# The scan stage of a hybrid diffusion step on one Trainium2 core: decay sums spread over the partitions by TensorE, exponentials with a bias on ScalarE, one 1024-column product on VectorE

## The chip, the cores and the metric

The kernel runs on one core of a Trainium2 chip. The core has five engines that run side by side, each with its own instruction stream in order: TensorE (PE: matmuls; its weight loads, PEld, are a row of their own in the profile), VectorE (DVE), ScalarE (ACT), GpSimd (POOL) and SyncE (SP, which issues most DMAs). They meet only in semaphores. The metric is the device time of one execution in microseconds, lower is better; the median of three runs before is 1650.7 us (1649.86 to 1651.47).

## The reference, cut to what matters

One layer works on 640 tokens (128 context, 512 latent), 5 chunks of 128. The stage that is changed is the two-way Mamba-2 scan: 32 heads of 64 columns in 4 groups of 8, state size 128. Per chunk, head and direction it computes

```
a_cs = cumsum(a)                                   # a = dt * a_neg, over the 128 tokens of a chunk
decay[t, s] = exp(a_cs[t] - a_cs[s])  for s <= t, else 0
y_diag = ((C B^T)[t, s] * decay[t, s]) @ (x * dt)  # 128x128 matrix per head and direction
y_off  = (C @ h_in) * exp(a_cs)                    # state that came into the chunk
state  = B^T @ (x * dt * exp(a_end - a_cs));  h = h * exp(a_end) + state
y = y_forward + y_backward + x * d_skip
```

The backward direction is the same with the tokens reversed, so its matrix is non-zero for s >= t. The rest of the layer (gMLP, convolution, projections, the mixture of experts) is not touched.

## The kernel before

The kernel is a chain of stages, each a block that begins and ends with a barrier of all engines: gMLP, branch A, convolution, gates, the scan (`stage_ssd`, L865), the norm behind it, branch B, the output projection, routing, the experts, and the combination. Order inside a stage is written out by hand, engine by engine, with semaphore counts.

The scan stage has a first part of 20 state products (L1029 and L1026, with POOL and DVE weighting rows of X, L936, and DVE carrying states, L1163 and L1166), and then a loop over 40 steps ("subs"): chunks 4, 3, 2, 1, 0, four groups each, and two halves `q` of 4 heads. What one step j does:

- POOL, `decays` (L983): two products 128x512, the low parts of a times a triangular mask, forward and backward. ACT, `decays` (L1121): eight copies 128x128 of the mask scaled with a rounded a, the high parts.
- PE, `prepare(j)` (L1040): four matmuls with 512 columns in one bank; they give a_cs[t] - a_cs[s] for 4 heads, both triangles in one 128x512 tile. Every second step it also makes C B^T of the group (L1048). PE does `prepare(j+1)` before it finishes step j.
- DVE, `masks` (L1197, L1198): C B^T times the lower and the upper mask, every second step. ACT exponentiates the bank (L1133) and scales the one mask product by dt of the forward direction (L1137, four times); DVE adds the other times dt of the backward direction (L1233, four times) and multiplies with the exponentials (L1239): the combined matrix M of 4 heads for both directions.
- PE: the state part C @ h of both directions (L1090, L1091), not in the last 8 steps (chunk 0), then waits for `matrix_ready` and makes y with M as the stationary operand (L1095, four matmuls of 128 columns, each on the X of two heads, of which one half is used). An f32 matmul shows as two records in the profile.
- DVE, `take_y`: scales the state part (L1212), adds (L1217, L1222); POOL makes x * d_skip (L1006) and the last sum into X (L989).

Two more jobs are threaded into the loop: 12 state products of the backward direction (L1029, with L936, L1163, L1166) and 19 of the 24 pieces of the modulation vector (`modulate`, L1059 with 8 f32 matmuls of a 2-column stationary operand, L1061, and the copy L1172 on DVE), which depend on nothing else in the loop but share PSUM bank 4 with C B^T: `modulate` waits for `cb_masked`.

## Time and profile before

| what | before |
|---|---|
| median of 3 runs | 1650.7 us |
| profiled execution, its own time | 1647.13 us |
| its span | 1645.4 us |
| mean granted TensorE clock | 0.913 of full |
| PE / PEld / DVE / ACT / POOL busy in the span | 1369.0 / 1188.6 / 920.8 / 693.6 / 279.6 us |
| the scan's loop: start of its first L1040, start of its last L1095 | 717.79 us, 960.47 us |

The span is from the first to the last instruction; the profiled execution's own time is 1.7 us longer. The granted clock is the share of full speed at which TensorE ran: it has two levels, full (2.4 GHz) and half (1.2 GHz), and a mean between them says how much of a stretch was at either. Matmuls are pipelined, so the distance between the starts of two blocks tells what one of them takes from PE, rather than the duration printed with it. A row of the timeline that has xN joins N records of one line. In the waits, the engine and line on the left sat idle until the engine and line on the right released it.

### The profile page before, as it was taken

The numbers are of one execution on the slowest core, as the hardware profiler recorded it, in microseconds if no ns is written. First come the engines' busy times: TensorE is split into PE (matmuls) and PEld (weight loads), VectorE is DVE, ScalarE is ACT, GpSimd is POOL, SyncE is SP. The second block draws the span as 40 slices with busy tenths as digits, with TensorE's granted clock in tenths as the row PEclk, the third lists the DMA queues.
The fourth block names the chain that finished last, engine by engine and source line by source line (L and its number), as shares of the span: only waits on it lengthen the run. The fifth ranks groups of instructions, "written<-read, shape, count | busy, mean of one in ns | idle before, by whom it ended". The sixth has DMA issues, their size and how long they took to land. (4 is left out here: it accounts for less than half of the span.)

```text
span 1645.4 us, 20520 instructions
## 1 busy us (share of the span) xinstructions
PE 1369.0 (83%) x7697; PEld 1188.6 (72%) x7697; DVE 920.8 (56%) x1201; ACT 693.6 (42%) x1186; POOL 279.6 (17%) x286
## 2 busy tenths in 40 slices
PE   3999989799998999787778734999974489999980
PEld 1799989799997889645555523998873378888860
DVE  2411532476762111288889868233346189999966
ACT  2423311244342221335557747111121177777753
POOL 0600000000000010256667741000004000000002
PEclk9999999899999999898889966999966799999995
DMA  9972211121213331511111131332435589999945
GB/s 385 406 305 77 76 53 52 59 74 57 78 52 109 118 134 72 170 52 39 39 40 40 51 140 60 115 101 92 162 153 195 201 314 408 406 412 413 413 186 204
DMA packets 55498, 267.96 MB, mean 163 GB/s; under 512 B 7467, under 2 KB 11763, under 8 KB 35062
## 3 DMA queue, kind: packets, MB, share of 16 engines
q1 hardware_dynamic: 42806, 221.21, 35.8%
q0 software_dynamic: 12608, 45.62, 7.1%
q8 instruction: 55, 0.90, 0.2%
q14 instruction: 29, 0.24, 0.0%
HBM read 218.54 MB, written 48.27 MB: 162 GB/s over the span
## 5 line engine op out<-in xcount | busy, mean ns | idle before, releaser
L212 PE MATMUL banks<-rounded,rounded 128*128 128x320 f32 (+1 forms) x1168 | 366.5, 314 | 20.2 <-PEq L1266 6.8
L213 PE MATMUL banks<-rounded,rounded 128*128 128x320 f32 (+1 forms) x1168 | 364.5, 312 | 0.0
L214 PE MATMUL banks<-rounded,rounded 128*128 128x320 f32 (+1 forms) x1168 | 364.4, 312 | 0.0
L191 DVE TENSOR_TENSOR rounded<-words,rounded 128x2048 fp32r<-128x2048 f32 x52 | 119.2, 2292 | 226.5 <-ACT rounded L183 224.3
L212 PEld LDWEIGHTS banks<-rounded,rounded 128*128 128x128 f32 (+1 forms) x1168 | 221.5, 190 | 21.8 <-issue 14.4
L1849 DVE TENSOR_TENSOR rounded<-words,rounded 128x2048 fp32r<-128x2048 f32 x93 | 212.9, 2290 | 34.3 <-ACT rounded L1840 33.4
L213 PEld LDWEIGHTS banks<-rounded,rounded 128*128 128x128 f32 (+1 forms) x1168 | 221.5, 190 | 0.4
L214 PEld LDWEIGHTS banks<-rounded,rounded 128*128 128x128 f32 (+1 forms) x1168 | 221.3, 189 | 0.4
L1840 ACT ACTIVATE rounded<-words 128x2048 fp32r<-128x2048 f32 x96 | 183.7, 1917 | 48.0 <-PE banks L1967 40.7
L183 ACT ACTIVATE rounded<-words 128x2048 fp32r<-128x2048 f32 x52 | 99.2, 1909 | 141.0 <-PE banks L233 62.6
L231 PE MATMUL banks<-rounded,rounded 128*128 128x512 f32 x280 | 112.1, 400 | 10.7 <-PEq L632 6.6
L232 PE MATMUL banks<-rounded,rounded 128*128 128x512 f32 x280 | 111.3, 398 | 0.0
L233 PE MATMUL banks<-rounded,rounded 128*128 128x512 f32 x280 | 111.1, 397 | 0.0
L1965 PE MATMUL banks<-rounded,rounded 128*128 128x512 f32 x256 | 103.1, 403 | 2.8 <-issue 2.4
L1966 PE MATMUL banks<-rounded,rounded 128*128 128x512 f32 x256 | 101.5, 397 | 0.0
L1967 PE MATMUL banks<-rounded,rounded 128*128 128x512 f32 x256 | 101.4, 396 | 0.0
L854 POOL DMA_DIRECT2D silu_z<-words x20 | 10.9, 543 | 531.4 <-ACT words L834 531.4
L1121 ACT ACTIVATE rounded<-words,rounded 128x128 fp32r<-128x128 f32 x320 | 97.2, 388 | 0.0
L1233 DVE SCALAR_TENSOR_TENSOR words<-words,words 128x128 f32<-128x128 f32 x160 | 92.6, 636 | 2.6 <-ACT words L1137 2.6
L983 POOL TENSOR_TENSOR rounded<-words,words 128x512 fp32r<-128x512 f32 x80 | 89.1, 1134 | 22.3 <-PE banks L1040 22.3
L1095 PE MATMUL banks<-words,words 128*128 128x128 f32 x320 | 51.2, 310 | 48.2 <-DVE words L1239 48.2
L1095 PEld LDWEIGHTS banks<-words,words 128*128 128x128 f32 x320 | 45.0, 213 | 59.6 <-DVE words L1239 48.2
(269 smaller groups left out, 2227.7 us busy)
## 6 DMA issues: line engine op xcount, KB each, us to landing
words<-in_units SPq DMA_DIRECT2D x52, 1024.0 KB, 5.0
words<-in_wg SPq DMA_DIRECT2D x32, 1024.0 KB, 7.4
words<-in_wu SPq DMA_DIRECT2D x32, 1024.0 KB, 7.5
words<-in_wd SPq DMA_DIRECT2D x32, 1024.0 KB, 8.3
words<-in_w_mod_rest SPq DMA_DIRECT2D x32, 512.0 KB, 4.9
slot_rows<-words POOLq DMA_DIRECT2D x27, 512.0 KB, 22.9
expert_rows<-words POOLq DMA_DIRECT2D x25, 512.0 KB, 9.0
words<-in_w_mod SPq DMA_DIRECT2D x4, 2048.0 KB, 22.5
```

What stands on the lines that cost most here:

```text
L191: self.nc.vector.tensor_tensor(self.lo[:, i % 2, :], self.raw[:, i % 2, :], self.hi[:, i % 2, :].bitcast(F32), ALU.subtract).then_inc(self ...
L212: nc.tensor.matmul(out, lhs[0](k), rhs[0](k), start=(k == 0), stop=False)
L213: nc.tensor.matmul(out, lhs[0](k), rhs[1](k), start=False, stop=False)
L214: last = nc.tensor.matmul(out, lhs[1](k), rhs[0](k), start=False, stop=(k == nk - 1))
L231: nc.tensor.matmul(out, rows[0], w[0][:, k, :], start=(kk == 0), stop=False)
L232: nc.tensor.matmul(out, rows[0], w[1][:, k, :], start=False, stop=False)
L233: last = nc.tensor.matmul(out, rows[1], w[0][:, k, :], start=False, stop=(kk == KD - 1))
L1840: self.nc.scalar.activation(self.hi[:, q % 3, :], self.raw[q], ACT.Copy).then_inc(self.hi_ready, 1)
L1849: (ops or self.nc.vector).tensor_tensor(self.lo[:, q % 3, :], self.raw[q], self.hi[:, q % 3, :].bitcast(F32), ALU.subtract).then_inc(self. ...
L1965: nc.tensor.matmul(o, HB[0][:, kk, :], hi[:, cols], start=(kk == 0), stop=False)
L1966: nc.tensor.matmul(o, HB[0][:, kk, :], lo[:, cols], start=False, stop=False)
L1967: last = nc.tensor.matmul(o, HB[1][:, kk, :], hi[:, cols], start=False, stop=(kk == KD - 1))
```

## The change

The two triangles are no longer put in one tile. For each direction a bank of PSUM first gets a constant from a bf16 matmul of the identity with a tile `shut` (0 where the mask lets through, -BIG elsewhere, 512 columns), and then, per head, an f32 matmul whose stationary operand is one column of a repeated 128 times and whose moving operand is the mask (128 columns): this puts a_cs[t] on all partitions. ACT's exponential then takes the bank with a bias per partition, the negated sum -a_cs[s] (`NCS`, two new copies at the start of the stage), so that exp(a_cs[t] - a_cs[s]) comes out, and 0 outside of the triangle: eight ACT instructions 128x128 per step, into `E`, three steps deep. DVE multiplies all 1024 columns of E with C B^T (`CB`, now a plain copy by ACT out of PSUM) in one instruction. dt goes to the rows of X (`XT`, POOL, `time_rows`, 512 columns per step), and since the two directions have their own matrices and rows, y takes eight f32 matmuls of 64 columns that accumulate in pairs. The high and low parts of a, the masks product, the dt scalings on ACT and DVE and the rounding at the start of the stage are gone. The state part is scaled in one DVE instruction (`scale_off`), taken as soon as PE has made it; POOL adds x * d_skip and the backward state part, and makes the last sum.

```diff
-    RH, RL = kit.rnd(O_HL + 2048, 4, 512), kit.rnd(O_HL + 4096, 4, 512)
-    GX, TT = (kit.at(O_HL + 6144 + 1024 * j, 2, 512) for j in range(2))
+    E = kit.at(O_HL + 2048, 6, 512)
+    XT = kit.at(O_HL + 5120, 6, 256)
...
 PE
             def prepare(j):
                 c, g, q = subs[j]
-                pe.wait_ge(low_decays, 2 * j + 2)
-                if j >= 2:
-                    pe.wait_ge(seg_exp, j - 1)
-                pe.wait_ge(high_decays, 8 * (j + 1))
-                for n, (mask, R) in enumerate(((gtr, RH[:, j % 2, :]), (gtr, RL[:, j % 2, :]),
-                                               (ltr, RH[:, 2 + j % 2, :]), (ltr, RL[:, 2 + j % 2, :]))):
-                    last = nc.tensor.matmul(ps[:, j % 2, :], mask, R, start=(n == 0), stop=(n == 3))
-                last.then_inc(seg_done, 1)
+                for d, mask in ((0, le), (1, ge)):
+                    if j:
+                        pe.wait_ge(decays_done, 8 * j - 4 + 4 * d)
+                    nc.tensor.matmul(ps[:, d, :].rearrange("p (h n) -> p h n", h=4), identb,
+                                     shut[:, d, :].unsqueeze(1).broadcast_to([P, 4, P]), start=True, stop=False)
+                    for h in range(4):
+                        n = 32 * d + heads4(g, q).start + h
+                        last = nc.tensor.matmul(ps[:, d, h * P:(h + 1) * P], A[:, c, n:n + 1].broadcast_to([P, P]), mask,
+                                                start=False, stop=(h == 3))
+                    last.then_inc(sums_spread, 1)
...
+                pe.wait_ge(rows_timed, j + 1)
                 pe.wait_ge(matrix_ready, j + 1)
                 for h in range(4):
-                    x0 = g * GW + q * 256 + (h // 2) * P
-                    last = nc.tensor.matmul(ps[:, 2 + j % 2, h * P:(h + 1) * P], M[:, j % 2, h * P:(h + 1) * P],
-                                            X[:, c, x0:x0 + P], start=True, stop=True)
+                    o = ps[:, 2 + j % 2, h * HD:(h + 1) * HD]
+                    for d in range(2):
+                        b = 2 * (j % 3) + d
+                        last = nc.tensor.matmul(o, E[:, b, h * P:(h + 1) * P], XT[:, b, h * HD:(h + 1) * HD],
+                                                start=(d == 0), stop=(d == 1))
                 last.then_inc(y_done, 1)
...
 ACT
-            nc.scalar.activation(AH, A, ACT.Copy).then_inc(a_split, 1)
             act.wait_ge(sums_done, 1)
+            for n in range(2):
+                nc.scalar.activation(NCS[:, n, :, :].rearrange("p c h -> p (c h)"), ps[:, n, 0:160],
+                                     ACT.Copy, scale=-1.0).then_inc(exps_done, 1)
...
+            for j, (c, g, q) in enumerate(subs):
+                if j >= 3:
+                    act.wait_ge(y_done, j - 2)
+                for d in range(2):
+                    if d and q == 0:
+                        gi = j // 2
+                        act.wait_ge(cb_done, gi + 1)
+                        if gi >= 2:
+                            act.wait_ge(matrix_ready, 2 * (gi - 1))
+                        nc.scalar.activation(CB[:, gi % 2, :], ps[:, 4, (gi % 2) * P:(gi % 2 + 1) * P], ACT.Copy).then_inc(cb_taken, 1)
+                    act.wait_ge(sums_spread, 2 * j + d + 1)
                     for h in range(4):
-                        hs = 32 * d + heads4(g, q).start + h
-                        nc.scalar.activation(RH[:, 2 * d + j % 2, h * P:(h + 1) * P], mask, ACT.Copy,
-                                             scale=AH[:, c, hs:hs + 1].bitcast(F32)).then_inc(high_decays, 1)
+                        n = heads4(g, q).start + h
+                        nc.scalar.activation(E[:, 2 * (j % 3) + d, h * P:(h + 1) * P], ps[:, d, h * P:(h + 1) * P], ACT.Exp,
+                                             bias=NCS[:, d, c, n:n + 1]).then_inc(decays_done, 1)
...
 DVE
-                for h in range(4):
-                    dt = DT[:, c, 32 + g * HPG + 4 * q + h:32 + g * HPG + 4 * q + h + 1]
-                    tt = TT[:, j % 2, h * P:(h + 1) * P]
-                    nc.vector.scalar_tensor_tensor(out=tt, in0=CB[:, (j // 2) % 2, 1, :], scalar=dt, in1=tt,
-                                                   op0=ALU.mult, op1=ALU.add).then_inc(both_scaled, 1)
...
-                nc.vector.tensor_tensor(M[:, j % 2, :], TT[:, j % 2, :], GX[:, j % 2, :], ALU.mult).then_inc(matrix_ready, 1)
+                dve.wait_ge(cb_taken, j // 2 + 1)
+                dve.wait_ge(decays_done, 8 * j + 8)
+                e = E[:, 2 * (j % 3):2 * (j % 3) + 2, :].rearrange("p d (h t) -> p (d h) t", h=4)
+                nc.vector.tensor_tensor(e, e, CB[:, (j // 2) % 2, :].unsqueeze(1).broadcast_to([P, 8, P]),
+                                        ALU.mult).then_inc(matrix_ready, 1)
...
 POOL
+                nc.gpsimd.tensor_tensor(XT[:, 2 * (j % 3):2 * (j % 3) + 2, :].rearrange("p d (h n) -> p d h n", h=4),
+                                        rows.unsqueeze(1).broadcast_to([P, 2, 4, HD]),
+                                        dt.unsqueeze(3).broadcast_to([P, 2, 4, HD]), ALU.mult).then_inc(rows_timed, 1)
```

What this makes of TensorE's instructions in one step of the loop. Before, one step on TensorE, from its `prepare` (L1040) through a state product (L1029), a modulation piece (L1059, L1061), the state part (L1090, L1091) to y (L1095):

```order
L1040 MATMUL banks<-rounded_2048_5415,rounded_128_5417 128x512
L1040 MATMUL banks<-rounded_2048_5416,rounded_128_5417 128x512
L1040 MATMUL banks<-rounded_2048_5415,rounded_128_5418 128x512
L1040 MATMUL banks<-rounded_2048_5416,rounded_128_5418 128x512
L1029 MATMUL banks<-words_52992_59,words_28160_54 128x512
L1059 MATMUL banks<-words_42496_49,words_33280_56 2x128 x8
L1061 MATMUL banks<-words_42496_49,words_52992_59 2x128
L1090 MATMUL banks<-words_10240_52,words_28160_54 128x256
L1091 MATMUL banks<-words_10240_52,words_28160_54 128x256
L1095 MATMUL banks<-words_20480_55,words_50688_5414 128x128 x4
```
After, the same step; L1038 is the bf16 matmul of the constant, L1042 the spread sums, L1030, L1062, L1064, L1094 and L1095 are the old L1029, L1059, L1061, L1090 and L1091, and L1102 is y:

```order
L1038 MATMUL banks<-words_33280_56 128x512
L1042 MATMUL banks<-words_52992_59,words_33280_56 128x128 x4
L1038 MATMUL banks<-words_33280_56 128x512
L1042 MATMUL banks<-words_52992_59,words_33280_56 128x128 x4
L1030 MATMUL banks<-words_52992_59,words_28160_54 128x512
L1062 MATMUL banks<-words_42496_49,words_33280_56 2x128 x8
L1064 MATMUL banks<-words_42496_49,words_52992_59 2x128
L1094 MATMUL banks<-words_10240_52,words_28160_54 128x256
L1095 MATMUL banks<-words_10240_52,words_28160_54 128x256
L1102 MATMUL banks<-words_50688_5414 128x64 x8
```
Nothing has changed its place. Four matmuls of 512 columns have become two of 512 and eight of 128, and four of 128 columns have become eight of 64.

On VectorE, one step and its surroundings before (words_33280_56 holds C B^T, the scales and the state part, words_50688_5414 the exponentials and the matrices):

```order
L1233 SCALAR_TENSOR_TENSOR words_50688_5414<-words_33280_56,words_50688_5414 128x128 x4
L1239 TENSOR_TENSOR words_50688_5414<-words_50688_5414 128x512
L1212 TENSOR_TENSOR words_33280_56<-banks,words_33280_56 128x256 x2
L1217 TENSOR_TENSOR words_42496_49<-banks,words_33280_56 128x2x64 x2
L1222 TENSOR_TENSOR words_42496_49<-words_42496_49,words_33280_56 128x256
L1172 COPY words_42496_49<-banks 2x128
L1163 TENSOR_TENSOR words_42496_49<-words_10240_52,words_33280_56 128x512
L1166 TENSOR_TENSOR words_50688_5414<-words_42496_49,banks 128x512
```
and after, where L1214 is the product, L1194 the scaling of the state part, L1204 the sum that takes y, and L1169, L1160 and L1163 the modulation's copy and the carrying of a state:

```order
L1214 TENSOR_TENSOR words_50688_5414<-words_50688_5414,words_33280_56 128x1024
L1194 TENSOR_TENSOR words_33280_56<-banks,words_33280_56 128x512
L1204 TENSOR_TENSOR words_42496_49<-banks,words_33280_56 128x256
L1169 COPY words_42496_49<-banks 2x128
L1160 TENSOR_TENSOR words_42496_49<-words_10240_52,words_33280_56 128x512
L1163 TENSOR_TENSOR words_50688_5414<-words_42496_49,banks 128x512
```
Ten instructions of a step are three, and the scaling of a step's state part stands ahead of the sum that takes the y of the step before.

On ScalarE at the start of the stage, before:

```order
L1102 ACTIVATE words_33280_56<-words_33280_56 128x16
L1103 ACTIVATE rounded_320_5419<-words_33280_56 128x320
L1106 ACT_TABLE_LOAD
L1106 ACTIVATE words_33280_56<-banks 128x480 x2
L1112 ACTIVATE words_50688_5414<-banks 128x512 x8
```
and after (L1112 are the negated sums, L1115 the exponentials of the sums, L1121 the context states, L1136 the exponentials with a bias):

```order
L1109 ACTIVATE words_33280_56<-words_33280_56 128x16
L1112 ACTIVATE words_33280_56<-banks 128x160 x2
L1115 ACT_TABLE_LOAD
L1115 ACTIVATE words_33280_56<-banks 128x480 x2
L1121 ACTIVATE words_50688_5414<-banks 128x512 x8
```
The load of the exponentials' table stood ahead of everything that needs the sums; it now stands behind two copies that need them.

## Rows read from the trace of the kernel before

**Rows 1.** Windows: loop and its parts; stretch, length, busy us (xinstructions), clock, DMA share, GB/s
```profile
718.00:962.00 244.00, 185.99 (x1014) 135.03 (x1013) 210.38 (x460) 160.05 (x504) 159.20 (x161) 0.91 0.13 40
718.00:876.00 158.00, 121.80 (x610) 87.44 (x609) 134.91 (x279) 96.91 (x304) 98.43 (x103) 0.87 0.13 41
876.00:962.00 86.00, 64.19 (x406) 47.60 (x404) 75.47 (x182) 63.14 (x202) 60.77 (x59) 1.00 0.12 38
```
**Rows 2.** Waits in the loop, 718 to 962 us: total us, times, longest
```profile
ACT words L1133 <- PE banks L1040: 96.4, 31, 20.3
...
PE banks L1095 <- DVE words L1239: 48.2, 26, 3.3
...
PE banks L1059 <- DVE words L1198: 7.6, 9, 2.2
```
**Rows 3.** Groups of the loop: out<-in, shapes, xcount | busy us, mean ns | idle before
```profile
L1233 DVE SCALAR_TENSOR_TENSOR words<-words,words 128x128 f32<-128x128 f32 x160 | 92.6, 636 | 2.6 <-ACT words L1137 2.6
L1121 ACT ACTIVATE rounded<-words,rounded 128x128 fp32r<-128x128 f32 x304 | 92.5, 388 | 0.0
L983 POOL TENSOR_TENSOR rounded<-words,words 128x512 fp32r<-128x512 f32 x77 | 84.8, 1121 | 22.3 <-PE banks L1040 22.3
...
L1137 ACT ACTIVATE words<-words 128x128 f32<-128x128 f32 x160 | 50.8, 390 | 3.2 <-DVE words L1198 1.6
...
L1239 DVE TENSOR_TENSOR words<-words 128x512 f32<-128x512 f32 x40 | 32.5, 813 | 1.4
...
L989 POOL TENSOR_TENSOR words<-words,words 128x256 f32<-128x256 f32 x32 | 30.1, 942 | 0.0
```
**Rows 4.** Timeline of PE in the loop: start us, us, line, out<-in, xrecords [idle before]
```profile
874.39 1.02 PE L1029 MATMUL banks<-words,words 128*128 128x512 f32 x2
875.25 0.59 PE L1090 MATMUL banks<-words,words 128*128 128x256 f32 x2
...
880.76 1.91 PE L1059 MATMUL banks<-words,words 128*2 128x128 f32 x16 [2.21 <-DVE words L1198]
...
882.91 0.70 PE L1090 MATMUL banks<-words,words 128*128 128x256 f32 x2
883.44 0.59 PE L1091 MATMUL banks<-words,words 128*128 128x256 f32 x2
884.01 1.16 PE L1095 MATMUL banks<-words,words 128*128 128x128 f32 x8
884.93 1.19 PE L1040 MATMUL banks<-rounded,rounded 128*128 128x512 f32 x4
885.95 0.59 PE L1090 MATMUL banks<-words,words 128*128 128x256 f32 x2
```
**Rows 5.** Timeline of PE: first block and last block of the loop
```profile
717.79 1.19 PE L1040 MATMUL banks<-rounded,rounded 128*128 128x512 f32 x4
...
960.47 1.36 PE L1095 MATMUL banks<-words,words 128*128 128x128 f32 x8 [2.41 <-DVE words L1239]
```
**Rows 6.** Timeline of PE: f32 stationary operands 128x128 with 2 and 16 moving columns
```profile
28.73 1.05 PE L338 MATMUL banks<-words,words 128*128 128x2 f32 x8
...
1206.45 3.43 PE L1484 MATMUL banks<-words 128*128 128x16 f32 x16
```
**Rows 7.** Windows around the blocks of rows 6, for their clock
```profile
28.70:29.80 1.10, 1.08 (x12) 0.97 (x8) 0.00 (x0) 0.60 (x1) 0.00 (x0) 1.00 0.98 417
1206.00:1210.00 4.00, 4.00 (x21) 4.00 (x20) 0.24 (x1) 0.00 (x0) 0.00 (x0) 0.50 0.00 0
```
**Rows 8.** Timeline of ACT at the start of the stage
```profile
675.48 1.28 ACT L1106 ACT_TABLE_LOAD   x1
676.85 1.03 ACT L1106 ACTIVATE words<-banks 128x480 f32<-128x480 f32 x2
```
**Rows 9.** The instructions of L1552: duration ns min/median/max, first and last start
```profile
L1552 DVE TENSOR_TENSOR words<-words,words x5: 1224/1224/1225, 1196.2 to 1221.0; 128x1024 f32<-128x1024 f32 x5
```

More of the change, by code:

```diff
@@ L915, in stage_ssd @@
     NS, NL = len(subs), 32
-    ev = lambda j: 5 * j if j <= NL else 5 * NL + 2 * (j - NL)
     ctx_states = [(d, 0, g) for d in range(2) for g in range(G)]
@@ L975, in _, with time_rows @@
         def _(pool):
-            def decays(j):
+            def time_rows(j):
                 c, g, q = subs[j]
-                if j >= 2:
-                    pool.wait_ge(seg_done, j - 1)
-                for d, mask in ((0, le), (1, ge)):
-                    hs = heads4(g, q)
-                    av = A[:, c, 32 * d + hs.start:32 * d + hs.stop]
-                    nc.gpsimd.tensor_tensor(byhead(RL[:, 2 * d + j % 2, :], 4), av.unsqueeze(2).broadcast_to([P, 4, P]),
-                                            mask.unsqueeze(1).broadcast_to([P, 4, P]), ALU.mult).then_inc(low_decays, 1)
+                if j >= 3:
+                    pool.wait_ge(y_done, j - 2)
+                hs = heads4(g, q).start
+                rows = byhead(X[:, c, g * GW + q * 256:g * GW + (q + 1) * 256], 4)
+                dt = DT[:, c, :].rearrange("p (d h) -> p d h", d=2)[:, :, hs:hs + 4]
+                nc.gpsimd.tensor_tensor(XT[:, 2 * (j % 3):2 * (j % 3) + 2, :].rearrange("p d (h n) -> p d h n", h=4),
+                                        rows.unsqueeze(1).broadcast_to([P, 2, 4, HD]),
+                                        dt.unsqueeze(3).broadcast_to([P, 2, 4, HD]), ALU.mult).then_inc(rows_timed, 1)
@@ L1090, in _ @@
                     nc.tensor.matmul(ps[:, 5 + j % 2, 0:256], ct, hF[:, c - 1, w4], start=True, stop=True)
[L1091 removed]
+                    nc.tensor.matmul(ps[:, 5 + j % 2, 256:512], ct, hb(c)[:, w4], start=True, stop=True).then_inc(off_done, 1)
+                pe.wait_ge(rows_timed, j + 1)
                 pe.wait_ge(matrix_ready, j + 1)
                 for h in range(4):
[L1094 to L1096 removed]
+                    o = ps[:, 2 + j % 2, h * HD:(h + 1) * HD]
[3 more added lines that the diff above has]
+                                                start=(d == 0), stop=(d == 1))
                 last.then_inc(y_done, 1)
@@ L1200, in take_y @@
             def take_y(j):
                 c, g, q = subs[j]
-                w4 = slice(g * GW + q * 256, g * GW + (q + 1) * 256)
-                v = ps[:, 2 + j % 2, :].rearrange("p (a n) -> p a n", a=2)
-                n = ev(j)
                 dve.wait_ge(y_done, j + 1)
-                dve.wait_ge(skip_ready, j + 1)
-                dst = V1[:, j % 2, :] if c else X[:, c, w4]
-                if c and j >= 2:
-                    dve.wait_ge(y_whole, j - 1)
+                v = ps[:, 2 + j % 2, 0:256]
@@ L1220, in take_y @@
-                if c:
-                    dve.wait_ge(y_steps, n + 4)
-                    nc.vector.tensor_tensor(dst, dst, OF[:, j % 2, 0, :], ALU.add).then_inc(y_steps, 1)
-            masks(0)
-            for j, (c, g, q) in enumerate(subs):
-                if j % 2 and j + 1 < NS:
-                    masks((j + 1) // 2)
-                dve.wait_ge(upper_scaled, 4 * j + 4)
-                dve.wait_ge(cb_masked, 2 * (j // 2) + 2)
-                for h in range(4):
-                    dt = DT[:, c, 32 + g * HPG + 4 * q + h:32 + g * HPG + 4 * q + h + 1]
-                    tt = TT[:, j % 2, h * P:(h + 1) * P]
-                    nc.vector.scalar_tensor_tensor(out=tt, in0=CB[:, (j // 2) % 2, 1, :], scalar=dt, in1=tt,
-                                                   op0=ALU.mult, op1=ALU.add).then_inc(both_scaled, 1)
-                dve.wait_ge(both_scaled, 4 * j + 4)
-                dve.wait_ge(seg_exp, j + 1)
-                if j >= 2:
-                    dve.wait_ge(y_done, j - 1)
-                nc.vector.tensor_tensor(M[:, j % 2, :], TT[:, j % 2, :], GX[:, j % 2, :], ALU.mult).then_inc(matrix_ready, 1)
+                    dve.wait_ge(off_scaled, j + 1)
@@ new lines, in take_y @@
+                    nc.vector.tensor_tensor(V1[:, j % 2, :], v, OF[:, j % 2, 0, :], ALU.add).then_inc(y_steps, 1)
+                else:
+                    dve.wait_ge(skip_ready, j + 1)
+                    nc.vector.tensor_tensor(X[:, c, g * GW + q * 256:g * GW + (q + 1) * 256], v, YK[:, j % 2, :],
+                                            ALU.add).then_inc(y_steps, 1)
+            for j, (c, g, q) in enumerate(subs):
+                dve.wait_ge(cb_taken, j // 2 + 1)
[3 more added lines that the diff above has]
+                                        ALU.mult).then_inc(matrix_ready, 1)
+                if c:
+                    scale_off(j)
```

119 lines of the change are left out of this document (46 added, 73 removed).

## The prediction

> **What bounds the kernel now.** I read the loop of the scan stage, since all of the edit but its first lines is there. First the windows: in 244 us of loop VectorE is busy 210.4 us (86%), TensorE 186.0 at a mean granted clock of 0.91, ScalarE 160.1, GpSimd 159.2 [rows 1]. Then the waits, to see who holds whom: TensorE waits 48.2 us in front of y (L1095) for VectorE's product L1239, ScalarE waits 96.4 us for the next bank from TensorE, TensorE waits 7.6 us in front of the modulation for VectorE's masks [rows 2]. So the loop runs at VectorE's pace, 244/40 = 6.1 us a step, and TensorE, with a quarter of its time idle, is next. The chain of waits over the whole kernel ends outside of the stage; it says nothing here. Since every stage ends with a barrier, what the loop loses or gains shows in full in the total.
>
> The obvious reading is that VectorE, ScalarE and GpSimd are relieved and the loop gets shorter. The question is what TensorE's work becomes, because it is the only engine that gets more.
>
> **The other engines.** VectorE sheds L1233 (92.6 us) and L1239 (32.5 us) [rows 3] and gains 40 products of 1024 columns. The nearest row is a 128x1024 f32 tensor product at 1.224 us [rows 9], so 49 us; bounds 0 and twice this. 210 - 125 + 49 = 134 us, at most 183. The scaling of the state part and the adds only get fewer instructions; I take nothing for them. ScalarE sheds L1121 (92.5) and L1137 (50.8) and gains 320 exponentials 128x128; the same size takes 388 to 390 ns there [rows 3], so 125 us, and 20 copies, 8 us: 160 - 143 + 133 = 150 us, and the 40 old exponentials are in it still. GpSimd sheds L983 (84.8), gains 40 products of 512 columns at 1.12 us (45) and 32 adds at 0.94 (30) [rows 3]: 150 us. If TensorE takes 255 us or more, all three are covered. If that cover goes, the next is VectorE or ScalarE at 150 to 180, far below today's 244.
>
> **TensorE's work, added to what it has.** Today: 186.0 busy at a mean clock of 0.91 is 186 x 0.91 = 169 us at full clock [rows 1].
> - y: a block of 8 records (4 f32 matmuls, 128x128 stationary, 128 columns) takes 884.93 - 884.01 = 0.92 us, 0.115 a record [rows 4]. The new one has 8 matmuls with 64 columns, 16 records, each with a stationary operand of its own. Does half of the columns make a record half as long? Two blocks have almost no moving columns: 8 records with 2 columns take 1.05 us with their tail at full clock, at most 0.131 each; 16 with 16 columns take 3.43 us at half clock, 0.214 each, which is 0.107 at full [rows 6, 7]. So an f32 stationary operand of 128 columns costs 0.107 to 0.131 however little moves over it. I take 0.112: 16 x 0.112 = 1.79 us, 0.9 us more a step. From below: by moving columns alone, 256 of them take 0.53 to 0.57 us in two records (883.44 - 882.91 and 884.01 - 883.44) [rows 4], so 64 would take about 0.07 a record.
> - prepare: four records of 512 columns take 885.95 - 884.93 = 1.02 us, 0.255 each [rows 4]. Now two bf16 matmuls of 512 columns (priced as those: 0.51; from below 0, a stationary operand in bf16 may load faster, from above 0.51 each as the f32 L1029 with 0.86 us for two records [rows 4] suggests) and 8 f32 matmuls with 128 columns, 16 records at 0.112 = 1.79: 2.30 us, 1.28 more. That the stationary operand is one column repeated changes nothing that I can price: even if its load were free, 128 moving columns take as long (the modulation's 18 records with a stationary operand of 2 columns take 2.15 us, 0.119 each [rows 4]).
> - Together 2.18 us a step, 40 steps: 87 us. 169 + 87 = 256 us at full clock.
>
> A second way to the same number, from the blocks: 40 x (2.30 + 1.79) = 164; state part 32 x 1.10 (882.91 to 884.01) = 35; modulation 19 x 2.15 (880.76 to 882.91) = 41; states 12 x 0.86 (874.39 to 875.25) = 10; C B^T 20 x 2 x 0.115 = 5 [rows 4]. Sum 255.
>
> The Trainium skill has both sides of this in "TensorE: Matmul & The Clock Gate". Section "LDWEIGHTS (loading the stationary operand)": a load's time goes by the columns of the stationary operand, over 1.2 GHz; for 128 that is 107 ns, and the blocks with 2 and 16 moving columns agree. Section "Back-to-back issue gap": alone, a matmul takes its moving columns over 2.4 GHz and 2.5 ns. By that rule a record of the new y would take well under 0.1 us; that is the second rival below.
>
> **What TensorE still waits for.** prepare(j+1) waits for the exponentials of step j, one bank at a time. From its start T: sums of the first direction to T+1.15, their four exponentials to T+2.8 (at 0.39), the copy of C B^T behind them to T+3.2, the other four to T+4.8, the product to T+6.0, or T+7.2 at twice its price. TensorE's y of that step comes at T + one step (1.79 + 2.30 + 1.10 = 5.2) + 2.30 + 1.10 = T+8.6. So the product is early, except in the last 8 steps, which have no state part: y there at T+4.1+2.3 = T+6.4, a wait of 0 to 0.8 us, 8 times; I take 0. In the first step there is no such distance: about 1 us. And the modulation still waits for C B^T, now for ScalarE's copy, behind four exponentials. This bites in the 9 of 19 pieces that sit in odd steps, where C B^T has only just been made: T+2.5 when TensorE is there, T+3.3 when the copy is done; 0.7 x 9 = 6 us (7.6 today [rows 2]; from 0 to 9 x 2.2 = 20 [rows 4]).
>
> Loop: 256 + 1 + 6 = 263 us, say 264, at full clock. The loop today is from 717.79 to 960.47 + 1.36 = 961.83, 244 us [rows 5]. **Difference +20 us.** The granted clock: I take full, since the second part of today's loop has 1.00 with TensorE busy 64 of 86 us [rows 1], and the new one will be idle 7 of 264.
>
> **The start of the stage.** Today the table load of 1.28 us stands before the sums are there and hides; then two ACTIVATEs follow, 0.5 us each, that DVE's scales and with them all weighting wait for [rows 8]. Now two copies of 160 columns (0.3 each, between the 0.39 of 128 columns and half of that) and then the table load come first: 1.28 + 0.6 = 1.9 us on the path. The rounding of a and its subtraction go, but they ran beside the same wait. **+1.9 us.** ScalarE no longer makes 16 copies ahead of the loop; nobody waited for them.
>
> **Sum.** 1647.13 + 20 + 2 = 1669 for the profiled execution; it lay 3.6 us under the median of the runs, so 1650.7 + 22 = 1672.7. I say **1672 us**. Spread of the terms: 32 records a step at 0.107 instead of 0.112 is -6 us, at 0.126 +18; waits for the copy 0 to 20, that is -6 to +14.
>
> **Rivals.**
> 1. TensorE is the bound, but its clock stays at today's mean of 0.91. 256/0.91 + 7 = 288, +44 +2: 1697. For it: from 718 to 876 us the clock is 0.87 with TensorE busy three quarters of the time. Against: the same busy share has 1.00 from 876 on [rows 1], and gaps in front of y are what goes. The skill says in the same page ("Part 1: The HAM clock gate") that activity releases the throttle; by that the denser loop is at full clock. Chance 12%.
> 2. Faster: records of y cost what moves over them, 0.07 us or a little less. 16 x 0.06 = 0.96 in place of 1.79, 0.83 x 40 = 33 us less: loop 231, -13 + 2: 1640. It decides if 16 records of y take under 1.3 us, since 264 - 40 x 0.5 = 244. For it: VectorE's bound surely goes, and all else has room. Against: the two blocks of rows 6. With the chance that the added sums hide in some other way: 10%.
> 3. Lock step: the distance of one step between sums and product does not cover exponentials, copy and product (all of them slower than their rows), and TensorE waits about 1 us in front of each y: +40, 1713. Against: the 2.6 us of room above. It would need a product of 3 us or more. 6%.
> 4. Both cancel, within 0.2% (3.3 us, about what a measurement of this kernel can tell from no change): 4%.
>
> My forecast has 68%. Slower 68 + 12 + 6 = 86%, same 4%, faster 10%. The range goes from the low end of the terms, 1672 - 12 = 1660, a little further towards no change, 1658, to the clock rival's 1697; that leaves about 2 in 10 outside.
>
> **What would show it.** TensorE idle in the loop under 15 us, weight loads busy nearly all of it, y's block at 1.7 to 1.9 us and the spread sums of a direction at 0.9 us behind 0.25; granted clock 1.00; VectorE's largest idle group released by TensorE or ScalarE in front of L1214; a loop of about 264 us; a table load after the negated sums. I am wrong if y's block takes 1.3 us or less, if the loop's clock is below 0.97, or if TensorE waits for L1214 in most steps.

## The result and the profile after

The changed kernel takes 1660.37 us (four runs, 1658.74 to 1661.19) against 1650.86: ratio 1.0057, interval 1.004 to 1.0074. Measured again beside other runs of both it was 1657.11 against 1650.77, ratio 1.0045, 1.0031 to 1.0058. It is slower, as forecast, but by 6 to 10 us and not by 21.

| | before | after | forecast |
|---|---|---|---|
| start of the scan stage to its loop | 44.5 us | 47.1 us | +1.9 |
| loop, start of its first block to end of its last y | 244.0 | 253.8 | 264 |
| both | 288.6 | 300.9 | +22 |

Inside the stage the two profiles differ by 12.4 us. The rest of the profiles' difference, and the distance to the medians, is other stages, whose code is the same in both kernels: this stage began 673.3 and 675.0 us into the span in two profiles of the kernel before, 674.8 and 669.7 in two of the changed one.

The window of the loop, as in [rows 1]: stretch, length, busy us of PE, PEld, VectorE, ScalarE, GpSimd, clock.

```profile
721.90:975.70 253.80, 248.39 (x1895) 215.48 (x1894) 105.73 (x156) 92.89 (x340) 155.82 (x153) 1.00 0.12 39
```
TensorE is busy 248.4 of 253.8 us and at full clock throughout, where it was at 0.91. VectorE falls from 210 us to 106, ScalarE from 160 to 93, GpSimd stays (159 to 156). The waits of TensorE, as in [rows 2]:

```profile
PE banks L1062 <- ACT words L1132: 4.1, 9, 0.5
PE banks L1102 <- DVE words L1214: 0.9, 1, 0.9
PE banks L1038 <- ACT words L1136: 0.2, 1, 0.2
```
and three of the other engines, from a window a little wider:

```profile
ACT words L1136 <- PE banks L1042: 178.5, 40, 25.0
DVE words L1194 <- PE banks L1095: 117.2, 32, 6.4
...
DVE words L1214 <- ACT words L1136: 15.1, 5, 3.5
```
The 48.2 us in front of y are 0.9, and now VectorE and ScalarE wait for TensorE. One step of the loop without other jobs, and the first and last blocks, to compare with [rows 4, 5]:

```profile
721.90 0.39 PE L1038 MATMUL banks<-words 128*128 128x512 bf16 x1
...
730.13 0.70 PE L1094 MATMUL banks<-words,words 128*128 128x256 f32 x2
730.66 0.59 PE L1095 MATMUL banks<-words,words 128*128 128x256 f32 x2
731.10 1.89 PE L1102 MATMUL banks<-words 128*128 128x64 f32 x16
732.83 0.38 PE L1038 MATMUL banks<-words 128*128 128x512 bf16 x1
733.04 1.05 PE L1042 MATMUL banks<-words,words 128*128 128x128 f32 x8
733.93 0.38 PE L1038 MATMUL banks<-words 128*128 128x512 bf16 x1
734.15 1.05 PE L1042 MATMUL banks<-words,words 128*128 128x128 f32 x8
735.04 0.39 PE L1051 MATMUL banks<-words 128*128 128x128 f32 x2
735.26 0.60 PE L1094 MATMUL banks<-words,words 128*128 128x256 f32 x2
```
...and the end:

```profile
973.73 1.97 PE L1102 MATMUL banks<-words 128*128 128x64 f32 x16 [0.92 <-DVE words L1214]
```
y takes 732.83 - 731.10 = 1.73 us, 0.108 for each of 16 records, though half as many columns move as in the 0.115 of [rows 4]. prepare takes 735.04 - 732.83 = 2.21 us where it took 1.02. The whole step is 735.26 - 730.13 = 5.13 us. The start of the stage, beside [rows 8]:

```profile
678.36 0.50 ACT L1112 ACTIVATE words<-banks 128x160 f32<-128x160 f32 x2 [1.72 <-PE banks L1068]
678.87 1.28 ACT L1115 ACT_TABLE_LOAD   x1
680.17 1.03 ACT L1115 ACTIVATE words<-banks 128x480 f32<-128x480 f32 x2
```
The table load stands behind the negated sums, as the order of the instructions said: from the sums to the end of their exponentials it takes 1.8 us more. And the groups that answer to [rows 3]:

```profile
L1136 ACT ACTIVATE words<-banks,words 128x128 f32<-128x128 f32 x320 | 89.4, 370 | 178.5 <-PE banks L1042 178.5
...
L1214 DVE TENSOR_TENSOR words<-words,words 128x1024 f32<-128x1024 f32 x40 | 53.4, 1335 | 15.1 <-ACT words L1136 15.1
L991 POOL TENSOR_TENSOR words<-words,words 128x256 f32<-128x256 f32 x32 | 49.4, 1542 | 64.3 <-DVE words L1204 64.0
```
The product of 1024 columns costs 1335 ns (1224 in [rows 9]), an exponential with a bias 370. Look at the last row: GpSimd's sum into X has 256 columns, as in [rows 3], and takes 1542 ns in place of 942.

### The profile page after: what moved, and what is told of

Read it like the earlier page. It is cut to its first block and busy times, and to the rows that moved or that the text cites. A ratio compares the mean times of both kernels' runs of the same rounds, so it can differ in the third digit from the quotient of the medians.

```text
span 1659.0 us, 21834 instructions
## 1 busy us (share of the span) xinstructions
PE 1436.3 (87%) x8577; PEld 1273.0 (77%) x8577; DVE 815.5 (49%) x897; ACT 621.9 (37%) x1007; POOL 276.0 (17%) x278
## 3 DMA queue, kind: packets, MB, share of 16 engines
q8 instruction: 62, 1.02, 0.2%
## 5 line engine op out<-in xcount | busy, mean ns | idle before, releaser
L1136 ACT ACTIVATE words<-banks,words 128x128 f32<-128x128 f32 x320 | 89.4, 370 | 178.5 <-PE banks L1042 178.5
L854 POOL DMA_DIRECT2D silu_z<-words x20 | 10.9, 543 | 532.5 <-ACT words L834 532.5
L779 DVE SCALAR_TENSOR_TENSOR words<-words 128x642 f32<-128x642 f32 x96 | 85.2, 888 | 3.4
L1042 PEld LDWEIGHTS banks<-words,words 128*128 128x128 f32 x640 | 84.0, 190 | 2.5
L1042 PE MATMUL banks<-words,words 128*128 128x128 f32 x640 | 84.3, 275 | 0.0
L1194 DVE TENSOR_TENSOR words<-banks,words 128x512 f32<-128x512 f32 x32 | 22.1, 692 | 117.2 <-PE banks L1095 117.2
```

What stands on the lines that cost most here:

```text
L1042: last = nc.tensor.matmul(ps[:, d, h * P:(h + 1) * P], A[:, c, n:n + 1].broadcast_to([P, P]), mask, start=False, stop=(h == 3))
```

## The experiments

All are variants of the changed kernel unless they say otherwise. "Loop" is measured in the run's trace as in the table.

**Is TensorE the bound, and what does a record cost?**

```diff
-                    for d in range(2):
-                        b = 2 * (j % 3) + d
-                        last = nc.tensor.matmul(o, E[:, b, h * P:(h + 1) * P], XT[:, b, h * HD:(h + 1) * HD],
-                                                start=(d == 0), stop=(d == 1))
+                    b = 2 * (j % 3)
+                    last = nc.tensor.matmul(o, E[:, b, h * P:(h + 1) * P], XT[:, b, h * HD:(h + 1) * HD],
+                                            start=True, stop=True)
```

> The changed kernel, with y made of the forward direction alone (the backward matrices and rows are still made, their four matmuls a step are left out). Theory: TensorE is the bound of the loop and a record with an f32 stationary operand of 128 columns costs 0.11 us whatever moves; 8 records a step less are 40 x 8 x 0.11 = 35 us: 1625 from the changed kernel's 1660. Rival (a record costs its 64 moving columns, and something else paces the loop): 8 x 0.06 x 40 = 19 us at most, 1641 or more. Rival (VectorE or ScalarE paces the loop): no change, 1660.

Measured: 1637.91 us, ratio 0.992 (0.9901 to 0.9938); loop 233.2. Of the 35 us expected in the loop 20.6 came, which is nearer to the 19 of the first rival. So this run does not separate the two. What the trace shows is that TensorE now waits:

```profile
PE banks L1030 <- POOL words L933: 9.9, 11, 1.1
...
PE banks L1101 <- DVE words L1213: 3.7, 10, 1.8
```
The timeline around one such wait, GpSimd and TensorE together:

```profile
761.96 1.52 POOL L991 TENSOR_TENSOR words<-words,words 128x256 f32<-128x256 f32 x1
...
762.61 1.05 PE L1042 MATMUL banks<-words,words 128*128 128x128 f32 x8
...
763.44 1.04 POOL L933 TENSOR_TENSOR words<-words,words 128x512 f32<-128x512 f32 x1
...
764.53 1.12 PE L1030 MATMUL banks<-words,words 128*128 128x512 f32 x2 [0.87 <-POOL words L933]
```
TensorE is done with prepare at about 763.5 (1.05 us with its tail from 762.61) and starts the state product at 764.53, as soon as GpSimd's weighting L933 has ended at 764.48. L933 could not start before GpSimd's sum L991 of the step before had ended. The rows of waits count from the modelled end of the block before, tail and all, so they show less than is lost: 0.87 us here, while the start comes 1.92 us after that of prepare's last block in place of 0.89, which is 1.03 us, in most of the eleven.

```diff
-                    o = ps[:, 2 + j % 2, h * HD:(h + 1) * HD]
+                    o = ps[:, 2 + j % 2, h * P:(h + 1) * P]
...
-                        last = nc.tensor.matmul(o, E[:, b, h * P:(h + 1) * P], XT[:, b, h * HD:(h + 1) * HD],
+                        last = nc.tensor.matmul(o, E[:, b, h * P:(h + 1) * P], XT[:, b, (h // 2) * P:(h // 2 + 1) * P],
```

> The changed kernel, with 128 moving columns in place of 64 in each of the eight y matmuls of a step (the rows of two heads, half of the result unused, taken by two adds on VectorE in place of one). Theory (the load of the stationary operand sets the record): 0.112 us a record in place of 0.110, 0 to +2 us, 1660 to 1662. Rival (the moving columns set the record): a record gets 0.05 us longer, +34 us, 1694.

Measured: 1662.23 us, ratio 1.0072 (1.0052 to 1.0093); loop 256.0, +2.2. Twice the moving columns cost 0.0034 us a record, so they do not set it; the rival is out. That it is the load of the stationary operand fits TensorE's weight loads, which have rows of their own (the changed kernel's loop, loads of 128 columns for y and of 2 for the modulation):

```profile
L1102 PEld LDWEIGHTS banks<-words 128*128 128x128 f32 x640 | 77.1, 192 | 3.4 <-issue 1.7
L1062 PEld LDWEIGHTS banks<-words,words 128*2 128x2 f32 x304 | 24.4, 84 | 19.6 <-issue 13.2
```
The load of 128 columns takes 192 ns in the mean, that of 2 columns 84: 126 columns are 108 ns, which is what a record of y takes. No block here has few columns on both sides, so that a record has a fixed price of the same size is not tested.

**The two small terms.**

```diff
-        at_sub[i * NS // (NP - EARLY)] = EARLY + i
+        at_sub[2 * i] = EARLY + i
```

> The changed kernel, with the 19 modulation pieces of the loop in even steps 0, 2, ..., 36 only, so that none waits for the copy of C B^T that has just been made. Theory: the waits of TensorE in front of L1062 go, 4 us: 1656 to 1657. Rival (the wait was in the shadow of another): 1660.

Measured: 1653.68 us, ratio 1.0021 (1.0009 to 1.0034); loop 249.8, -4.0. The nine waits (4.1 us) were on the path.

```diff
             act.wait_ge(sums_done, 1)
-            for n in range(2):
-                nc.scalar.activation(NCS[:, n, :, :].rearrange("p c h -> p (c h)"), ps[:, n, 0:160],
-                                     ACT.Copy, scale=-1.0).then_inc(exps_done, 1)
             for n in range(2):
                 nc.scalar.activation(EX[:, 3 * n:3 * n + 3, :, :].rearrange("p a b c -> p (a b c)"), ps[:, n, 0:480],
                                      ACT.Exp).then_inc(exps_done, 1)
+            for n in range(2):
+                nc.scalar.activation(NCS[:, n, :, :].rearrange("p c h -> p (c h)"), ps[:, n, 0:160],
+                                     ACT.Copy, scale=-1.0).then_inc(exps_done, 1)
...
-            dve.wait_ge(exps_done, 4)
+            dve.wait_ge(exps_done, 2)
```

> The changed kernel, with the exponentials of the sums at the start of the stage ahead of the negated sums, and VectorE's scales waiting for the exponentials alone. The table load then stands ahead of what needs the sums, as before the change. Theory: the start of the stage gets back 1.9 to 2.6 us: 1658. Rival (the weighting of the first rows was not what the state products waited for): 1660.

Measured: 1658.01 us, ratio 1.005 (1.0034 to 1.0067). In the trace the part ahead of the loop is 44.4 us, as before the change (47.1 in the changed kernel), and the loop is 253.9: the whole start term is this order. The median alone could not have told it.

**Is the relief of the other engines worth nothing?**

```diff
+                nc.vector.tensor_tensor(spare, e[:, 0:4, :], CB[:, (j // 2) % 2, :].unsqueeze(1).broadcast_to([P, 4, P]),
+                                        ALU.mult).then_inc(spare_done, 1)
```

> The changed kernel, with a second product of 512 columns on VectorE in every step, behind the first and into a spare buffer, so that nothing of the result depends on it: 40 x 0.6 = 24 us more of VectorE's work. Theory (VectorE's relief was worth nothing, since TensorE is the bound and VectorE idles half of the loop): 0 to +3 us, 1660 to 1663. Rival (VectorE still paces part of the loop): up to +24 us, 1684.

Measured: 1667.92 us, ratio 1.0107 (1.009 to 1.0124); loop 263.0, +9.2: neither the theory's 0 to 3 nor the rival's 24. The added product takes 1.09 us in the mean and not 0.6. VectorE was busy 148.6 us of the 263.0, yet TensorE waited:

```profile
PE banks L1031 <- POOL words L934: 8.0, 11, 0.8
PE banks L1063 <- ACT words L1133: 4.1, 9, 0.5
```
The first row is new. Two things make it, and the rows of one step show both (lines are one higher here: L1220 is the added product, L1195 the scaling, L1205 VectorE's sum, L992 GpSimd's last sum, L934 the weighting):

```profile
760.93 0.68 DVE L1195 TENSOR_TENSOR words<-banks,words 128x512 f32<-128x512 f32 x1
...
763.17 1.03 DVE L1220 TENSOR_TENSOR words<-words,words 128x512 f32<-128x512 f32 x1
```
```profile
762.01 1.64 POOL L992 TENSOR_TENSOR words<-words,words 128x256 f32<-128x256 f32 x1 [0.43 <-DVE words L1205]
763.61 1.49 POOL L934 TENSOR_TENSOR words<-words,words 128x512 f32<-128x512 f32 x1
```
First the queue: y of that step starts at 760.26, and the scaling 0.67 us behind it, since the added product stands ahead of it; in the changed kernel it is 0.27 (762.59 to 762.86). GpSimd's last sum waits for VectorE's sum behind the scaling and ends 0.38 us later. Second, the weighting, whose code is the same, takes 1.49 us beside the added product where it takes 1.04 in the changed kernel (mean of the eleven 1.488 and 1.038). Together 0.83 us, and the state product comes 1.84 us after the start of prepare's last block in place of 1.01. The first and the last of the eleven lose less, 0.45 and 0.24; in all it is 8.2 of the 9.2.

In the changed kernel the same meeting has no room left. GpSimd's rows of one step:

```profile
763.96 1.64 POOL L991 TENSOR_TENSOR words<-words,words 128x256 f32<-128x256 f32 x1 [0.50 <-DVE words L1204]
765.56 1.04 POOL L933 TENSOR_TENSOR words<-words,words 128x512 f32<-128x512 f32 x1
```
and TensorE's at that time:

```profile
765.64 1.05 PE L1042 MATMUL banks<-words,words 128*128 128x128 f32 x8
766.65 1.12 PE L1030 MATMUL banks<-words,words 128*128 128x512 f32 x2
```
The weighting ends at 766.60, the state product starts at 766.65, and prepare would have let it start at about 766.53 (765.64 + 0.89). All eleven weightings of the loop end 0.05 us before their state product starts, so each of these is held up a little, about 1.4 us in all, and no row of waits shows it. The loop of the changed kernel is bound by TensorE, and GpSimd's chain already touches it. The product is not far off either. VectorE, from the last steps of one piece of its queue to the product of the next step:

```profile
757.83 0.69 DVE L1194 TENSOR_TENSOR words<-banks,words 128x512 f32<-128x512 f32 x1 [6.08 <-PE banks L1095]
758.43 0.41 DVE L1204 TENSOR_TENSOR words<-banks,words 128x256 f32<-128x256 f32 x1
758.77 0.27 DVE L1169 COPY words<-banks 2x128 f32<-2x128 f32 x1
758.96 0.67 DVE L1160 TENSOR_TENSOR words<-words,words 128x512 f32<-128x512 f32 x1
759.67 0.69 DVE L1163 TENSOR_TENSOR words<-words,banks 128x512 f32<-128x512 f32 x1
760.27 1.60 DVE L1214 TENSOR_TENSOR words<-words,words 128x1024 f32<-128x1024 f32 x1
```
The product ends at 761.87, and its y starts at 762.59: 0.7 us of room. Every second of the first 20 steps has under 1 us, the others 3.9 or 5.8, and most of the tight products take 1.60 us where the others take 1.22; the product stands behind the scaling, the sum, the modulation's copy and the carried state, all of which wait for TensorE's state part of the step before.

**Less work for TensorE.** The step sizes go into the bias of the exponential, so that y needs one matrix again:

```diff
+                nc.scalar.activation(NCS[:, n, :, :], DT[:, :, 32 * n:32 * n + 32], ACT.Ln).then_inc(logs_done, 1)
...
-                nc.vector.tensor_tensor(e, e, CB[:, (j // 2) % 2, :].unsqueeze(1).broadcast_to([P, 8, P]),
+                nc.vector.tensor_tensor(ef, ef, eb, ALU.add).then_inc(both_added, 1)
+                dve.wait_ge(both_added, j + 1)
+                nc.vector.tensor_tensor(ef, ef, CB[:, (j // 2) % 2, :].unsqueeze(1).broadcast_to([P, 4, P]),
                                         ALU.mult).then_inc(matrix_ready, 1)
...
-                        last = nc.tensor.matmul(o, E[:, b, h * P:(h + 1) * P], XT[:, b, h * HD:(h + 1) * HD],
-                                                start=(d == 0), stop=(d == 1))
+                    last = nc.tensor.matmul(o, E[:, 2 * (j % 3), h * P:(h + 1) * P], X[:, c, x0:x0 + HD],
+                                            start=True, stop=True)
```

> The changed kernel, with the step sizes put into the bias (log dt - sum, one logarithm per stage), so that the two directions' matrices can be added on VectorE (512 columns), multiplied with C B^T (512 columns) and used in 4 y matmuls of 64 columns straight on X; GpSimd's rows of X times dt go. 8 records a step less on TensorE, 35 us; the run with one direction showed that about 14 us of that come back as waits for the product and for GpSimd, and GpSimd is relieved here, VectorE is not. Theory: loop 222 to 230 us, 1629 to 1637, faster than both kernels. Rival (two dependent products on VectorE make y wait in each step): loop 240 us or more, 1647 or more.

Measured: 1635.95 us, ratio 0.9907 (0.9891 to 0.9924); loop 232.2. Within the expected time, two microseconds over the expected loop. TensorE waits 8.1 us for the product (3.7 in the first run with one direction) and 3.8 us for weighted rows (9.9 there). GpSimd's relief took 6 us from one wait, and the other grew by 4: 13 of the 35 us did not come, about as expected.

```diff
-                        last = nc.tensor.matmul(ps[:, d, h * P:(h + 1) * P], A[:, c, n:n + 1].broadcast_to([P, P]), mask,
-                                                start=False, stop=(h == 3))
+                        for k in range(3):
+                            last = nc.tensor.matmul(ps[:, d, h * P:(h + 1) * P], AB[:, k, n:n + 1].broadcast_to([P, P]), maskb[:, d, :],
+                                                    start=False, stop=(h == 3 and k == 2))
```

> The changed kernel, with a split in three bf16 parts and the masks in bf16, so that a spread sum takes 3 bf16 matmuls of 128 columns, one record each, in place of 1 f32 matmul of two records: 24 records a step in place of 16. Theory (a bf16 stationary operand of 128 columns loads behind 128 moving columns, 0.056 to 0.08 us a record): 1.35 to 1.9 us a step in place of 1.83, 0 to 19 us less, middle 1650. Rival (its load costs 0.11 us as in f32): +0.8 us a step, 1692.

Measured: 1648.91 us, ratio 0.998 (0.9963 to 0.9996); loop 242.9, -10.9.

```profile
807.77 0.38 PE L1049 MATMUL banks<-words 128*128 128x512 bf16 x1
807.99 0.83 PE L1054 MATMUL banks<-words,words 128*128 128x128 bf16 x12
808.66 0.38 PE L1049 MATMUL banks<-words 128*128 128x512 bf16 x1
```
Twelve bf16 records take 808.66 - 807.99 = 0.67 us, 0.056 each, half of an f32 record with the same 128 columns (0.89 us for eight above). 2 x 0.22 x 40 = 18 us of work gone, 11 of time: the rows show 4.5 us of new waits for weighted rows, and less than is lost, as above.

Now all that helped, together:

> All that should help together: step sizes in the bias, the logarithms behind the context copies so that no table load stands ahead of the exponentials of the sums, modulation pieces in even steps only, and the sums in three bf16 parts. Theory: the run with the bias alone, less 4 us for the pieces, 2 us for the start, and half of what the bf16 sums alone give or more, as waits begin to bind: 1610 to 1625. Rival (TensorE is no longer the bound and the chain from sums to product sets a step): about the time of the bias alone, 1629 or more.

Measured: 1622.44 us, ratio 0.9822 (0.9805 to 0.9838); loop 222.5, the part ahead of it 43.9. TensorE waits 13.7 us for the product and 7.9 for weighted rows.

**Do the weighted rows explain what came back?**

```diff
-                if j in x_at:
-                    weigh(pool, nc.gpsimd, x_at[j])
...
+                if j + 1 in x_at:
+                    weigh(pool, nc.gpsimd, x_at[j + 1])
                 if 1 <= j < NL + 1:
                     finish_y(j - 1)
```

> As the run with the forward direction alone (it leaves out the backward half of y), and GpSimd weights the rows of each state product one step earlier, ahead of its last sum of the step before. Theory (what came back there was TensorE waiting for these rows, since GpSimd's last sum stands before them and waits for VectorE's scaling of the state part): the 11 waits in front of the state product go, 10 to 11 us, and the loop is 222 to 224 us in place of 233; 1627. Rival (the time was lost to something else): loop 233, 1638.

Measured: 1628.59 us, ratio 0.9874 (0.986 to 0.9889); loop 220.5, 33.3 under the changed kernel's, where the records left out are worth 35.

```profile
PE banks L1063 <- ACT words L1132: 4.1, 9, 0.5
PE banks L1102 <- DVE words L1214: 3.6, 10, 1.8
```
The wait for GpSimd is gone, and with it 12.7 us of the loop. 33.3 us for 8 records a step is 0.104 each, so this run, unlike the first, is with the theory and out of the rival's reach.

The same order of GpSimd's work in the version with everything:

> All that should help, with the rows of the state products weighted one step earlier on GpSimd. Theory: the 8 to 10 us of waits in front of the state product go, the 14 us in front of y stay or take a part of it back: loop 213 to 218 in place of 222.5, 1614 to 1618. Rival (each wait that goes is replaced by one for the product in the same step): loop 222, 1622.

Measured: 1616.21 us, ratio 0.98 (0.9785 to 0.9814), the fastest version: 2% faster than the kernel before. Its loop is 215.5 us.

```profile
PE banks L1101 <- DVE words L1223: 16.8, 13, 1.6
PE banks L1036 <- ACT words L1135: 1.4, 1, 1.4
```
```profile
717.40:932.80 215.40, 197.00 (x1894) 154.66 (x1893) 126.42 (x197) 93.11 (x341) 111.18 (x113) 1.00 0.14 45
```
Of the 7.9 us in front of the state product about 3 moved to the product. The second row is a table load at the start of the loop (1.28 us from 718.44), which the logarithms between two groups of exponentials bring; the version with everything has it too. TensorE is still busy 197 of 215 us.

**The two kernels once more.**

> The changed kernel as it is, once more, for the size of the result: the first comparison gave +9.5 us in the median, the two profiles +12.4 us inside the stage. Theory (the stage's 12.4 is what the change costs, the rest is what the other stages do from run to run): 10 to 13 us slower than before. Rival: 7 to 9.

Measured: 1657.11 us, ratio 1.0045 (1.0031 to 1.0058). 6.3 us, less even than the rival's 7 to 9. Yet its profile has the same stage to 0.3 us: 46.9 and 253.8.

> The kernel before as it is, once more, for a second profile of its loop. Theory (the loop is paced by VectorE, half speed of TensorE in a sixth of it hides in TensorE's waits, and the pattern is that of the kernel): loop 243 to 245 us with 30 to 50 us of it at the half clock, as in the first profile. Rival (the first profile was a chance): another loop, by 3 us or more.

Measured: 1651.56 us, ratio 1.0006 (0.9996 to 1.0015), no difference. Its loop is 246.1 us, 2.1 more than in the first profile:

```profile
719.50:965.70 246.20, 188.37 (x1016) 137.00 (x1014) 210.88 (x459) 159.96 (x504) 157.68 (x161) 0.90 0.13 39
```
About 48 us of that loop are at the half clock, 42 in the first. So the stage before is 288.6 and 290.6 us in two profiles, after 300.9 and 300.7: the change costs 10 to 12 us there. Why the loop before varies and the one after does not is not tested; that it alone has half-clock stretches is what the windows show.

The medians say 9.5 and 6.3 us. Where the difference goes is not tested. The rest of the profiled executions, none of it touched, takes 1358.5 and 1363.7 us before and 1359.8 and 1354.8 after, so it moves by more than what is looked for. One part of it is steady: the stage behind the scan, from its first transfer to TensorE's first block of the next stage, takes 61.6 and 61.4 us before, 59.9 and 60.3 after. That is 1 to 2 us that the change seems to give back outside of its stage; the profiles show no cause.

## Why the prediction was wrong in size

The direction was right and so was the bound. What failed is the sum of TensorE's work, most of all its step "Together 2.18 us a step, 40 steps: 87 us". The range was wide enough to hold 1660.37 near its low end; that says nothing for the number.

- **TensorE becomes the bound: right.** It idles 5.4 us (253.80 less 248.39) where its waits were 56 [rows 2], at full clock, and the relief of VectorE and ScalarE is idle time. The clock rival (12%), the lock step rival (6%) and the one of no change (4%) did not come. Two of the signs came otherwise: VectorE's largest idle time, 117.2 us, is in front of its scaling and not of the product, and weight loads are busy 215 of 254 us, not nearly all.
- **An f32 record costs 0.107 to 0.131 however little moves: right.** 0.108 for 64 columns, 0.111 for 128 (wide y). By the Trainium skill's page "TensorE: Matmul & The Clock Gate", section "LDWEIGHTS (loading the stationary operand)", an estimate for 128 columns is 107 ns; the traces at full clock agree. That figure names no clock: at the half clock a record took 0.214 [rows 6, 7], and the measurement decides. The faster rival is refuted.
- **"Together 2.18 us a step, 40 steps: 87 us": the step that failed most.** Measured 1.19 for prepare (2.21 - 1.02, forecast 1.28) and 0.81 for y (1.73 - 0.92, forecast 0.90), 2.00 us a step, 80 us. I priced prepare's bf16 blocks at 0.255, the price of the old prepare's records with the change to the next block in it (they take 0.21 to 0.22: 3 us in 40 steps), y's records at 0.112 (they take 0.108: 2.4 us), and rounded 1.79 - 0.92 = 0.87 up to 0.9 (1.2 us).
- **The base of 169 us at full clock: it fits, but is not measured.** 248.4 busy less 80 is 168. That is a difference, and it hangs on 0.92 for the old block of y: ten steps before have that block at 0.81, start to start, and with it the rise is 84 us and the base 164. The work that was forecast at 256 and came as 248.4 is what the trace shows.
- **The second sum of 255 agreed by luck.** It has the same blocks of 164 us (now 3.94 x 40 = 158), and the state part at 1.10 us where its pair takes 0.97 in one half of the steps (731.10 - 730.13) and 0.87 in the other: 6 us too much.
- **Waits of 1 + 6 us:** measured 5.2. Removing the nine waits gave 4.0 us. The sum of 263 was called 264, one more.
- **Start of the stage +1.9:** measured 2.6; undone by the order of four instructions.
- So 264 should have been 254, and the stage +12 in place of +22. The target is a small difference of two large numbers: 7 us of 256 is 3%, and it was a third of the answer.
- **The other engines:** forecast 134, 150 and 150 us for VectorE, ScalarE and GpSimd, measured 106, 93 and 156. ScalarE's exponentials were priced at the 0.39 us that one lasts, but they overlap: 320 of them keep it busy 89.4 us, 0.28 each.
- **"All three are covered": all but true for the forecast, wrong as reasoning.** Busy sums (134 to 183 us against 255) said there was room; the queue order said otherwise. VectorE's scaling of the state part now stands ahead of its sum, that ahead of GpSimd's last sum, and that ahead of the weighted rows that TensorE wants a step later. I looked only at the product, priced from its inputs, with 2.6 us of room; behind the same queue it has 0.7 in every second of the first 20 steps. Here both chains cost little, about 1.4 us in front of the state products and 0.9 in front of y; but together they took 14 of 35 us in the first experiment, and the one through GpSimd 9 us when VectorE got 1.09 us more a step. GpSimd's sum at 0.94 us, where it takes 1.54, is a price in that chain that the forecast had wrong without harm.

## What to carry to other kernels

Price a change on the engine that gets more work, not on those that get less; for f32 matmuls in which no more than 128 columns move over a stationary operand of 128, count stationary operands rather than columns (0.108 to 0.112 us a record here; with 256 moving columns it is 0.43 us for two). When TensorE is the only busy engine, look for the chain through the slower queues that meets it just in time: its room decides how much of the next saving arrives, and it is read from ends and starts: busy sums and rows of waits did not show that it was used up here. And a forecast of 20 us made from 40 equal steps needs each step to 0.05 us, taken from the start-to-start distance of the very kind of block.

## What the runs showed of the hardware

GpSimd's sum of two SBUF tensors with 256 columns takes far longer beside VectorE's long product, the same form in both kernels (ns min/median/max; first after, then before):

```profile
L991 POOL TENSOR_TENSOR words<-words,words x32: 1103/1636/1827, 737.4 to 939.6; 128x256 f32<-128x256 f32 x32
```
```profile
L989 POOL TENSOR_TENSOR words<-words,words x32: 721/776/1301, 736.6 to 934.3; 128x256 f32<-128x256 f32 x32
```
The same holds the other way: VectorE's product is 1.22 us in the median and 1.78 at worst. The run with more work for VectorE bears it out: nothing else was added, and GpSimd's weighting went from 1.038 to 1.488 us in the mean and its whole busy time in the loop from 155.8 to 170.4, with the same 153 instructions. That VectorE's work holds GpSimd up is thus shown; the other way round is read from rows alone, and by what it happens no run separates. The Trainium skill has the mechanism in "SBUF — State Buffer" (section "SBUF: two separate sides"): VectorE and GpSimd share a pair of ports, and when VectorE reads two SBUF tensors and GpSimd reads SBUF too, the one that starts first has it for its whole instruction. The rows don't contradict it: the sum is 0.86 us longer in the median, under the 1.22 us of one product, and the sum that starts at 763.96 beside the product of 763.80 to 765.02 ends 0.58 us after it. The repeated column as a stationary operand loads no slower than another: 0.112 us a record, the weight load 190 ns in the mean beside the 192 of y. In bf16 a record with it takes 0.056.
